# Attention heads summed, scaled and turned by token; the mixer's last units and state stores in another order

## The reference, cut to what matters

```python
a = p[:, :, 0] - lam * p[:, :, 1]                  # per head, after two softmaxes
o = einsum('bhqk,bkhe->bqhe', a, v_all)            # 8 heads, 128 features each
o = _rms(o, head_g) * (1 - lam_init)               # root mean square over the 128 features
y = (o.reshape(B, T, D_MODEL) @ w_o)
x = x + g1[:, None, :] * y
```

## Time and profile before

| | |
|---|---|
| median of three runs | 1470.3 us |
| the profiled execution's own time | 1470.15 us |
| its span, first to last instruction | 1468.4 us |
| mean granted TensorE clock | 0.998 |
| PE busy | 1444.8 us (98%) |
| DVE, POOL, ACT busy | 1048.7, 759.3, 427.6 us |
| mixer with its heads | about 93 to 250 us |
| attention with its output projection | about 857 to 1057 us |

### The profile page before, as it was taken

One profiled execution on the slowest core, in us unless ns is written; L12 is line 12 of the kernel. 1 busy time (PEld: TensorE's weight loads), 2 busy tenths in 40 slices (PEclk: granted clock), 3 DMA queues, 4 the chain that ended last, 5 costly groups with the idle time before them and its releaser, 6 DMA issues.

```text
span 1468.4 us, 29233 instructions
## 1 busy us (share of the span) xinstructions
PE 1444.8 (98%) x11236; PEld 1368.3 (93%) x11236; DVE 1048.7 (71%) x1862; ACT 427.6 (29%) x906; POOL 759.3 (52%) x513
## 2 busy tenths in 40 slices
PE   6999999999999999999999999999999999999999
PEld 4987899999999999999999887778999999999998
DVE  5897665567776877776688347886966779476698
ACT  5303454211110011112232147774421133111132
POOL 2445343555555455555545444567565556555554
PEclk9999999999999999999999999999999999999999
DMA  9573222244456544444222252231222222222222
GB/s 377 177 254 133 89 87 74 87 157 151 166 200 214 194 144 162 153 169 138 83 92 72 84 190 89 89 103 38 79 85 73 86 94 79 89 84 86 86 90 104
DMA packets 57531, 183.50 MB, mean 125 GB/s; under 512 B 6440, under 2 KB 9904, under 8 KB 57440
## 3 DMA queue, kind: packets, MB, share of 16 engines
q1 hardware_dynamic: 54432, 179.25, 35.7%
q10 hardware_dynamic: 3008, 3.01, 0.6%
HBM read 171.69 MB, written 10.55 MB: 124 GB/s over the span
## 4 chain that ended last, share of the span: by engine, by line
PE 90%; DVE 5%; issue 1%; DMA 1%; ACT 1%; POOL 0%; SPq 0%; ACTq 0%; DVEq 0%; POOLq 0%
PE psum L779 62%; PE psum L845 7%; PE psum L1054 7%; PE psum L1253 3%; PE psum L1345 1%; PE psum L1188 1%; DMA ada_first<-in_ada_w 1%; PE psum L1308 1%; PE psum L1060 1%; DVE w_ring L2581 1%; DVE act_lo L2013 1%; PE psum L1295 1%; PE psum L1291 1%; PE psum L790 1%; PE psum L816 1%
## 5 line engine op out<-in xcount | busy, mean ns | idle before, releaser
L658 POOL TENSOR_SCALAR w_hi<-raw 128x1024 fp32r<-128x1024 f32 (+1 forms) x168 | 192.0, 1143 | 574.4 <-PE psum L779 478.3
L662 POOL TENSOR_TENSOR w_lo<-raw,w_hi 128x1024 fp32r<-128x1024 f32 (+2 forms) x195 | 440.5, 2264 | 14.0
L779 PE MATMUL psum<-act_hi,w_hi 128*128 128x288 f32 (+1 forms) x1952 | 424.8, 299 | 1.3 <-issue 0.6
L779 PE MATMUL psum<-act_hi,w_lo 128*128 128x288 f32 (+1 forms) x1952 | 420.9, 297 | 0.0
L779 PE MATMUL psum<-act_lo,w_hi 128*128 128x288 f32 (+1 forms) x1952 | 420.5, 297 | 0.0
L779 PEld LDWEIGHTS psum<-act_hi,w_hi 128*128 128x128 f32 x1952 | 315.5, 190 | 6.4 <-issue 4.0
L779 PEld LDWEIGHTS psum<-act_hi,w_lo 128*128 128x128 f32 x1952 | 316.0, 189 | 0.0
L779 PEld LDWEIGHTS psum<-act_lo,w_hi 128*128 128x128 f32 x1952 | 315.3, 189 | 0.0
L779 PE MATMUL psum<-hid_both,w_hi 128*128 128x288 f32 x704 | 122.9, 297 | 0.0
L1960 DVE SCALAR_TENSOR_TENSOR psum<-ada_quad,cst,psum 128x512 f32<-128x512 f32 x168 | 112.8, 748 | 0.0
L779 PEld LDWEIGHTS psum<-hid_both,w_hi 128*128 128x128 f32 x704 | 103.5, 189 | 1.2 <-issue 1.2
(11 more groups left out here) (383 smaller groups left out, 2457.2 us busy)
## 6 DMA issues: line engine op xcount, KB each, us to landing
raw<-in_w_stream SPq DMA_DIRECT2D x153, 512.0 KB, 3.5
ada_quad<-in_ada_w SPq DMA_DIRECT2D x56, 512.0 KB, 4.5
raw<-in_w_down SPq DMA_DIRECT2D x32, 704.0 KB, 4.1
ada_first<-in_ada_w SPq DMA_DIRECT2D x8, 1024.0 KB, 14.2
ada_ring<-in_ada_w SPq DMA_DIRECT2D x14, 512.0 KB, 4.4
ada_more<-in_ada_w SPq DMA_DIRECT2D x10, 512.0 KB, 5.3
line_rep<-line SPq DMA_DIRECT2D x8, 352.0 KB, 4.5
line<-line_rep SPq DMA_DIRECT2D x8, 352.0 KB, 5.2
```

The source lines that it names most:

```text
L658: pool.tensor_scalar(hi, src, 1.0, 0.0, ALU.mult, ALU.add).then_inc(hi_split, 1)
L662: last = pool.tensor_tensor(lo[:, c:c + w], src[:, c:c + w], hi[:, c:c + w].bitcast(F32), ALU.subtract)
L779: last = mm(psum[:, b + half, 0:n_cols], weights[wp][:, k, :], parts[ap][:, k, half * HT:half * HT + n_cols], start=(k == 0 and n == 0), s ...
```

## The change

Attention output by token: in `att_values` the attention is the weight and the values move, so that a head's output has tokens on the partitions. Two banks take heads in turn, `o_bank(h) = 5 + h % 2`; the sample's 64 tokens go to bank 4, columns 384 to 512. `out_squares` (ACT, s = 2) takes five accumulating Squares and then three small operations on 128 x 5; `out_root` (DVE, s = 3) is a Newton step of three operations on 128 x 5; `out_norm` (ACT, s = 3) scales five tiles; `out_turn` (PE, s = 4, ahead of `att_turn`) transposes five tiles back into the same bank; `out_back` (ACT, s = 4) copies two pieces to SBUF. The sums on PE, the full-width Ln and Exp on ACT and the Newton step on POOL are gone. `att_turn` of s = 3 now waits for `out_back` of the head before. `query_second(2)` comes one step earlier on DVE, and `head_hi(0)` and `head_lo(0)` come earlier.

```diff
-            def att_sums(h):
-                pe.wait_ge(osq_ready, h + 1)
...
-                mm(psum[:, 6, :], mean_sq, tmp[:, 0, 0:TP], start=True, stop=True)
+            def out_turn(h):
+
+                pe.wait_ge(on_ready, h + 1)
+                pe.wait_ge(at_ready, min(5 * H, 5 * h + 7))
+                for j in range(4):
+                    pe.transpose(psum[:, o_bank(h), j * P:(j + 1) * P], hn[j], ident)
+                pe.transpose(psum[:, 4, 448:512], hn[4], ident[0:TS, 0:TS]).then_inc(o_turned, 1)
...
+            def out_squares(h):
                 sa.wait_ge(o_out, h + 1)
...
+                for j in range(TT):
+                    src = psum[:, o_bank(h), j * P:(j + 1) * P] if j < 4 else o_sample
+                    n = P if j < 4 else TS
+                    last = af(hn[j], src, ACT.Square, accum_out=ssq[0:n, j:j + 1])
+                steps(last)
                 steps.wait()
+                steps(af(z5, ssq, ACT.Identity, bias=EPSC, scale=1.0 / P))
+                steps.wait()
+                steps(af(y5, z5, ACT.Ln))
+                steps.wait()
+                af(y5, y5, ACT.Exp, scale=-0.5).then_inc(oy_ready, 1)
+
+            def out_norm(h):
+                sa.wait_ge(of_ready, h + 1)
+                for j in range(TT):
+                    src = psum[:, o_bank(h), j * P:(j + 1) * P] if j < 4 else o_sample
+                    n = P if j < 4 else TS
+                    last = af(hn[j], src, ACT.Copy, scale=f5[0:n, j:j + 1])
+                last.then_inc(on_ready, 1)
+
+            def out_back(h):
+                sa.wait_ge(o_turned, h + 1)
...
+                af(o_place[h][:, 0:TP], psum[:, o_bank(h), :], ACT.Copy)
+                af(o_place[h][:, TP:T], psum[:, 4, 448:512], ACT.Copy).then_inc(ov_ready, 1)
...
+            def out_root(h):
+                ve.wait_ge(oy_ready, h + 1)
+                if h >= 1:
+                    ve.wait_ge(on_ready, h)
+                newton(y5, z5, t5, f5).then_inc(of_ready, 1)
```

Output projection: the last head's `out_turn` stands ahead of `out_part(15)`. The units after it use the bank pairs `o_banks = ((5, 7), (4, 6))`, and unit 4's tiles run in another order:

```diff
-            for k, j in ((0, 0), (0, 1), (1, 0), (1, 1), (2, 0), (3, 0), (2, 1), (3, 1)):
+            for k, j in ((0, 0), (1, 0), (2, 0), (0, 1), (1, 1), (2, 1), (3, 0), (3, 1)):
```

```diff
             project_values(U_V, A_IN, 0, between=between_values)
+            project(U_O, 0, act[0], bank=0, k1=1, free=lambda: wait_evac(pe, U_O + 1))
...
-            split_pairs(3, 26)
+            split_pairs(3, (U_OUT - 1) // 2)
+            split_behind(U_OUT + 2, lambda: pool.wait_ge(turned, H))
...
-                if h == H - 1:
-                    sa.wait_ge(state_out, 4)
...
+                for n, a in {4: ((0, 0),), 5: ((0, 1),), H - 1: ((1, 0), (1, 1))}.get(h, ()):
+                    sa.wait_ge(state_out, 2 * n + 2)
```

More of the change, by code:

```diff
@@ L1012, in _ @@
                     pe.wait_ge(evac[(U_O + h - 1) % 2], (U_O + h - 1) // 2 + 1)
-                project(U_O + h, 0, act[0], bank=0, k1=6)
+                project(U_O + h, 0, act[0], bank=0, k0=1 if h == 0 else 0, k1=6)
                 if h >= 1:
@@ L1357, in out_tile @@
                     for half in range(2):
-                        last = mm(psum[:, bank + half, 0:HT], w_parts[u % 2][wp][:, 4 * j + k, :],
+                        last = mm(psum[:, banks[half], 0:HT], w_parts[u % 2][wp][:, 4 * j + k, :],
                                   head_part(ap, 4 * part + k, half * HT, (half + 1) * HT),
@@ L1386, in _ @@
                     att_values(g - 3)
[L1387 to L1390, removed]
+                elif s == 4 and p >= 1:
+                    out_turn(p - 1)
                 if 1 <= g - 2 < 5 * H:
@@ L1417, in _ @@
             last.then_inc(unit_done, 1)
-            for n, banks in ((5, 4), (6, 4), (7, 0)):
+            for n in range(5, 8):
                 pe.wait_ge(lo_split, U_AO + n + 1)
@@ L1423, in _ @@
                     for k in range(4):
-                        last = out_tile(n, j, k, banks + 2 * j, n < 7 and k == 0, k == 3)
+                        last = out_tile(n, j, k, o_banks[j] if n < 7 else (2 * j, 2 * j + 1), n < 7 and k == 0, k == 3)
                     last.then_inc(unit_done if j else o_done, 1)
@@ L1833, in _ @@
                     att_by_key(g - 2)
-                late = p >= H - 2
                 if s == 2 and out:
                     out_sample(p - 1)
-                elif s == 3 and out and not late:
-                    z_sample(p - 1)
                 att_exp(g)
@@ L1841, in _ @@
                     query_z(p + 1)
-                elif s == 3 and late:
-                    z_sample(p - 1)
                 if s == 0 and p >= 1 and queries:
@@ L2547, in _ @@
                     att_weight(g - 1)
+                if s == 3 and p >= 1:
+                    out_root(p - 1)
                 if g == 3:
                     kq_scale(H + 1, tmp[:, 5, :])
+                    query_second(2)
                 elif s == 2 and 1 <= p < H - 1:
```

173 lines of the change are left out of this document (73 added, 100 removed).

## The result

The changed kernel takes 1479.6 us (median of 6 runs, 1478.4 to 1480.9), the one before 1470.3 (6 runs, 1468.4 to 1471.2): 0.64% slower, ratio 1.0064, 95% interval 1.0054 to 1.0075. The prediction said 1470.6 with a range up to 1475, so it was wrong. The profiled execution took 1479.5 us with a span of 1477.7, where before it was 1468.4: 9.3 longer.

A forecast was written before the change was run, and what follows sets the result against it. PE was taken to bound the kernel, busy 1444.8 of 1468.4 us. Attention +2.1 and mixer -1.8 gave +0.3 on the profiled 1470.15, so 1470.5; with the median 0.15 above, 1470.6 us, range 1464.5 to 1475.

The forecast's parts named there:

- PE asks for `out_turn` after 6.43 us: Attention heads 1 to 4: PE's way from the turn of s = 0 to its wait for ACT's scalings, 6.43 us.
- ACT is ready after 6.93: Same heads, same start: ACT's squares, small operations, exponentials and scalings end after 6.93 us, so PE waits 0.5 per head.
- Transposes 0.73 per head: PE in attention: five transposes of a head take 0.73 us as in the mixer, +5.8 us for eight heads.
- `out_back` makes the turn of s = 3 late, 0.2 per head: Heads 1 to 4: that turn waits for ACT's copy back, 0.2 us per head, +0.8 in all, bounds 0 and 0.5.
- Head 5 +1.5 net: Head 5: PE's way 5.27 us against ACT's 7.63, a wait of +2.4, less 0.5 of the old wait there.
- DVE's root is ready meanwhile: Attention, ACT's way to the scalings: DVE's Newton step finishes beside ACT's other work and adds no time.
- Heads 6 and 7 +1.4 each, less 2.0 of old waits: PE waits at `out_turn` for ACT, +2.8 us together; old waits for DVE's weighting and `part_to_x`, 2.0, go.
- the rival: POOL's splits slow DVE's weighting of s = 3: 0.7 us per head over seven heads, 1475.5 us; chance 0.19.
- Mixer -1.8: Mixer: filled wait ahead of the core -0.7, last head -0.3, unit 27's low part early -0.8 us.
- The rival "no effect": The mixer's edits do nothing: +1.8 us, 1472.4 us; chance 0.04.
- The rival on transposes at full duration: PE in attention: a head's five transposes cost 1.35 us instead of 0.73, +5.0, 1475.6 us; chance 0.03.
- No wait at out_turn: ACT's way is shorter, so PE does not wait for its scalings in attention: 1463.6 us, halfway 1466.5; chance 0.36.

The follow-up runs named there:

- attention alone: The changed kernel without its mixer edits, the mixer as in the kernel before: 1480.0 us, ratio to before 1.0073.
- high parts: The changed kernel with ACT's high parts of heads 3, 4 and 5 one step later, behind the five scalings: 1477.1 us, ratio to before 1.0052.
- tile order: The changed kernel with tile (3, 0) of unit 4 sixth of eight again, in place of seventh: 1477.6 us, ratio to before 1.0043.
- four pieces: The changed kernel with GpSimd's splits of the output projection's unit 3 and the next pair in four operations per part: 1474.6 us, ratio to before 1.0022.

## Why the prediction was wrong

- *PE asks for `out_turn` after 6.43 us*: measured 6.43. *ACT is ready after 6.93*: measured 7.10. The three small operations took 0.09 more than the 0.62 left for them, the start was 0.06 later, the five squares took 0.03 more; the rest fits. Wait 0.72 instead of 0.5: right mechanism, 0.9 us short over four heads. So what the prediction wanted to see in heads 1 to 4 was there, the turn of s = 2 in head 1 too (7.94 us, 7.72 forecast); it failed behind them.
- *Transposes 0.73 per head*: 0.79. The sample's values, taken as 0 with a bound of 0.5: 1.38 in place of 1.29 us, 0.7 over eight heads. The hidden wait of 0.16 went: twelve query matmuls take 1.73.
- *`out_back` makes the turn of s = 3 late, 0.2 per head*: half of it. No wait is listed there, but from the turn of s = 2 to that of s = 3 PE takes 2.57 us instead of 2.46. Heads 1 to 4: predicted +0.56 in all, measured +1.8.
- *Head 5 +1.5 net*: +1.4. That the late `head_hi` is a part of the wait is shown by moving it: 0.67 less.
- *"DVE's root is ready meanwhile"* is the step that failed, a term put at nothing. It was worked out for head 1 and used for all. In head 7 the whole split of unit 3 starts at 1009.31, just ahead of the root, and two of three tiny operations stand still, 2.8 us more than alone. *Heads 6 and 7 +1.4 each, less 2.0 of old waits*: head 6 waited 1.51, its old wait went, and it gave +0.5; head 7 has an idle time of 4.13. Holding the splits back, and cutting them, took 2.6 and 2.3 of it away. The earlier trace rows showed the very thing on a weighting in this head, and the rival priced it, but for pieces, over all heads and on the weighting; that the change put three new DVE operations on PE's path in the one head with a whole split was not seen. What that rival did name came in part, and cost nothing there: in heads 2, 3 and 4 a weighting of DVE takes 1.28, 1.51 and 1.41 us beside a split, where 0.55 or 0.75 was usual, and PE doesn't wait for it.
- The granted clock was in no term: 2.5 us behind the 4.13, which appears only when PE stands. *The last head: no wait*: 0.47, from the second whole split.
- *Unit 4's tile order +0.4*: 0.75, just above the bound of 0.7.
- *Mixer -1.8*: -0.6. The filler gave 0.58 of 0.7, the last head and unit 27 gave 0.38 of 1.1, since DVE's addition to x was next there with 0.54, and 0.32 was given back. It is the same mistake once more: the prediction feared GpSimd's high part on DVE there, and it was the low part, on an operation of 128x12. The rival "no effect" was nearer in size than the forecast.
- The rival on transposes at full duration is out, being right: 0.147 us apart, 0.27 long each. The Trainium skill ("TensorE: Matmul & The Clock Gate", Part 4: PE-mode transpose) gives about 275 ns for one; the trace has that as a duration, not as what one costs behind another.
- *No wait at out_turn*, 1463.6 by the forecast, was wrong for this order of work; with the wait taken away by a later `out_turn` the kernel stood at 1471.9, and with the blocks shortened at 1468.2, each in another set of runs.

Added up: 2.7 of wait beyond the 1.4, 2.5 of clock, 0.5 at the last head, 0.35 at unit 4, 1.3 in heads 1 to 4 and 1.2 in the mixer make 8.5 of the 9.0 us between forecast and result. Another 0.2 is the difference outside of the change.

Open: why the kernel before spreads in the later sets; whether the mixer's 1.2 come back when unit 27's split is cut or moved; and when a pause lets the clock fall, as below.

## What to carry to other kernels

An operation's size says nothing of its time beside GpSimd: before a chain is laid over DVE, look in the timeline for every GpSimd operation that can start while its small links run, in each head. Cut the long ones, or hold them back where the next DVE operation has time: that was worth 5.8 us in one order of work here and nothing in another. A wait on PE has to be priced with the clock behind it. When an engine is put between two pieces of PE's work, ask for its result a step later first; only then does the new form show what it is worth.

## What the runs showed of the hardware

A 128x5 operation of DVE with two inputs takes 0.17 us alone, 2.19 beside a GpSimd operation of 2.34, 0.33 beside pieces of 0.40 and 0.23 to 0.25 beside pieces half that size. One of 128x12 takes 0.17 alone and 1.84 beside an operation of 2.11.

The granted clock fell from 1.00 to 0.50 behind each of the four idle times of 4.1 us (the change, attention alone, high parts, tile order). Behind 2.32 us, at the same place, it fell in two traces (attention alone, four pieces) and not in three others; it fell behind 1.45, 1.73 (twice), 1.89 and 2.64 us, and stayed up behind 1.34, 1.51, 1.65, 1.79 and 2.41. So in these traces the length of the pause alone doesn't settle it. A fall was worth 1.3 to 2.5 us, and the two slowest of the changed kernel's six runs (1480.9 both) are the two with the lowest mean clock, 0.993 against 0.996 to 0.998. Comparisons under 2 us between kernels that differ by such a pause need the windows beside the times.
